# Eight transformer layers on one core: the boundaries between sublayers, taken token half by token half

## The chip, the cores and the metric

One core of a Trainium2 chip runs the whole program in one launch. The metric is the device time of one execution in microseconds (us), the median over runs. TensorE (PE) multiplies matrices, VectorE (DVE), ScalarE (ACT) and GpSimd (POOL) do the elementwise work, SyncE (SP) issues most of the transfers.

## What is computed

A residual stream x of 256 tokens by 1024 floats passes through ten sublayers, k = 0 to 9, all in float32. Sublayers 0 to 5 are two blocks of feed-forward, token mixer, feed-forward:

```
h = rms_norm(x, g_pre) * (1 + scale) + shift
y = sublayer(h)
x = x + res_w * (1 + gate) * rms_norm(y, g_post)
```

Sublayers 6 to 9 are attention, mixture of experts (MoE), attention, MoE. Their residual has no second norm:

```
h = rms_norm(x, g) * (1 + scale) + shift
x = x + gate * sublayer(h)
```

A feed-forward is (silu(h @ w_gate) * (h @ w_up)) @ w_down with a width of 2816; the mixers hold three kinds of attention and an output projection; the MoE has 16 experts of width 512, of which each token takes 2, and its router needs h of all tokens. Scale, shift and gate are vectors, made by a product of a second input with the "ada" weights.

## The kernel before

The 256 tokens are two halves t = 0, 1 of 128 rows each (NT = 2), which is also how `x[:, t, :]` lies in memory. All weights come as one stream of chunks of 1 MB (128 by 2048 floats) into six `stage` buffers. ACT makes the rounded high part of a chunk (`hi`, L578) and DVE the rest (`lo`, L1048), and each product is three matmuls on 512 columns (`mm3`, L1828, L1831, L1832). A high/low pair takes one of PARTS = 3 places, so `hi(n)` waits until PE is through with chunk n - 3.

A *column chunk* holds half of the contraction of a projection; `columns` takes it in 4 `mm3` groups for each token half, so 12 matmuls for each half and 24 in all. A *row chunk* (feed-forward down, output projection) is used by `rows`: for each token half t, 12 matmuls into the two PSUM banks `acc[2t]`, `acc[2t+1]`. When the last row chunk is done for t = 0, PE signals `half_done`.

At a boundary between sublayers k - 1 and k the engines do this, in the order in which their programs are written out (each engine is in order, nothing is scheduled at run time):

- **ACT** squares `acc` of t = 0 and of t = 1 to sums (L616, `pair<-acc`, sublayers 0 to 5 only), then x of t = 0 (L616, `pair<-x_tok`), then writes `x * rs` of t = 0 to `tok` in two parts (`by_root`, L964), then squares x of t = 1, and takes the high parts of h (`high(r)`, L980). `hi` of the next sublayer's second chunk was made before all this (`ahead`).
- **POOL** turns each sum into rs = (sum + eps) ** -0.5, by L550 and L553.
- **DVE** multiplies acc by the gate row (L1732, L1744), adds it to x (L1734, L1745), first t = 0, then t = 1; then for the four rounds r = 2t + half it takes the transposed quarter of x from PSUM with scale and shift (`scaled(r)`, L1687) and makes the low part (`rest(r)`, L1696), with `lo` of the second chunk between rounds 2 and 3.
- **PE** transposes `tok` in four rounds (`norm_round`, L1844). Three are in front of the first column matmul and the fourth is behind the first 12 matmuls (`normed`). Then come chunk 0 with both token halves and chunk 1 with both.

The last block of a feed-forward multiplies silu and product (L649, L1189), is transposed (L1892), is split in parts (L661, L1194), and is then taken by the last row chunk. Ahead of it, all of the row chunk before is done, both halves.

An MoE layer reads its chunks as float32 without a split, 96 of them, through twelve places: `stage` and the space of `w_hi` and `w_lo` (`w_raw`). Chunk 12 is loaded when PE has freed chunk 0 (`expert_chunk`). In its last expert pair ACT and DVE make parts of the next sublayer's first chunk between the last silu and the last results (`hi(end)`, L578, in `moe`).

SP issues the transfers in the order of the stream and waits at each for a free place; in the feed-forwards the slices of the ada weights (1 MB each) are laid between the chunks.

## Time and profile before

| what | value |
|---|---|
| median of 3 runs | 2297.01 us (2294.2 to 2298.27) |
| the profiled execution's own time | 2283.29 us |
| its span in the profile | 2281.3 us |
| PE busy | 2049.3 us, 90% of the span |
| DVE, ACT, POOL busy | 1438.7, 848.0, 67.6 us |
| L1048 `lo`, 240 times | 547.6 us |
| transfers | 592.53 MB, mean 260 GB/s |

A time line row reads: start in us from the span's start, duration in us, engine, line, operation, written tile <- read tiles, shapes, count; in brackets the idle time of the engine in front of it and what ended that. Rows that follow one another on one engine are merged (x2, x8), so a merged duration is that of the whole group. In matmul rows the duration covers the pipeline; the spacing of starts is what counts.

### The profile page before, as it was taken

How to read it: one execution, taken by the hardware profiler on the slowest of the kernel's cores; microseconds unless marked ns; L12 is line 12 of the kernel's file. 1: busy time of each engine (PE TensorE's matmuls, PEld its weight loads, DVE VectorE, ACT ScalarE, POOL GpSimd, SP SyncE). 2: the span in 40 equal slices, each digit the busy share in tenths (PEclk: the TensorE clock that was granted, in tenths of full speed). 3: DMA queues.
4: the chain of work that ended last, by engine and by line, in shares of the span. 5: the costliest groups of instructions: out<-in, count | busy, mean ns of one | idle time of the engine just before them, and what ended most of it. 6: DMA issues, size and time to landing. Idle time of an engine off the chain costs nothing.

```text
span 2281.3 us, 26827 instructions
## 1 busy us (share of the span) xinstructions
PE 2049.3 (90%) x9772; PEld 1513.4 (66%) x9772; DVE 1438.7 (63%) x2212; ACT 848.0 (37%) x1037; POOL 67.6 (3%) x93
## 2 busy tenths in 40 slices
PE   2999899988999899899988999886899879879997
PEld 2778788866887688778876788665544337654442
DVE  6888676656887888776656898676511137652111
ACT  3333545544343434554564433542200025321000
POOL 0000000000000000000000000110000001000000
PEclk9999999999999999999998999987999989999999
DMA  8999344334887699444432898341599985239997
GB/s 343 383 361 379 134 172 141 136 110 189 332 356 304 253 357 372 185 176 150 141 116 98 331 375 356 136 143 62 209 415 422 421 331 200 104 131 418 421 421 304
DMA packets 86332, 592.53 MB, mean 260 GB/s; under 512 B 9680, under 2 KB 13136, under 8 KB 15568
## 3 DMA queue, kind: packets, MB, share of 16 engines
q1 hardware_dynamic: 79760, 579.90, 64.3%
q10 hardware_dynamic: 6464, 11.15, 1.5%
q8 instruction: 73, 1.20, 0.2%
q14 instruction: 35, 0.29, 0.0%
HBM read 589.96 MB, written 1.05 MB: 259 GB/s over the span
## 4 chain that ended last, share of the span: by engine, by line
PE 71%; DMA 11%; DVE 10%; ACT 4%; issue 2%; POOL 1%; SPq 0%; ACTq 0%; DVEq 0%; POOLq 0%
PE acc L1828 12%; PE acc L1832 11%; PE acc L1831 11%; PE gu L2130 8%; PE gu L1828 6%; PE gu L1832 6%; PE gu L1831 6%; DMA w_raw<-wstream 5%; PE tr L2130 4%; DMA stage<-wstream 3%; PE acc L2130 3%; PE tr L1892 3%; DVE w_lo L1048 2%; DMA proj<-ada_stream 2%; DVE tf L1687 1%
## 5 line engine op out<-in xcount | busy, mean ns | idle before, releaser
L1048 DVE TENSOR_TENSOR w_lo<-stage,w_hi 128x2048 fp32r<-128x2048 f32 x240 | 547.6, 2286 | 68.0 <-ACT w_hi L578 67.9
L578 ACT ACTIVATE w_hi<-stage 128x2048 fp32r<-128x2048 f32 x240 | 457.4, 1911 | 279.1 <-PE acc L1832 261.3
L1120 DVE SCALAR_TENSOR_TENSOR proj<-proj,c_row 128x1024 f32<-128x1024 f32 x240 | 291.5, 1218 | 53.4 <-DMA proj<-ada_stream 44.7
L1828 PE MATMUL acc<-w_hi,hT_hi 128*128 128x512 f32 (+1 forms) x736 | 308.6, 419 | 5.1 <-DVE hT_lo L1392 5.1
L1828 PE MATMUL gu<-w_hi,hT_hi 128*128 128x512 f32 x704 | 283.8, 403 | 11.1 <-DVE pair L1189 10.8
L1831 PE MATMUL acc<-w_lo,hT_hi 128*128 128x512 f32 (+1 forms) x736 | 292.0, 397 | 0.0
L1832 PE MATMUL acc<-w_hi,hT_lo 128*128 128x512 f32 (+1 forms) x736 | 291.9, 397 | 0.0
L1832 PE MATMUL gu<-w_hi,hT_lo 128*128 128x512 f32 x704 | 277.7, 394 | 0.0
L1831 PE MATMUL gu<-w_lo,hT_hi 128*128 128x512 f32 x704 | 277.5, 394 | 0.0
L1828 PE MATMUL acc<-w_hi,yT_hi 128*128 128x512 f32 (+1 forms) x460 | 183.8, 400 | 14.0 <-DVE yT_lo L1604 5.7
L2130 PE MATMUL gu<-stage,got 128*64 128x512 f32 x768 | 170.6, 594 | 15.0 <-DMA stage<-wstream 15.0
L1832 PE MATMUL acc<-w_hi,yT_lo 128*128 128x512 f32 (+1 forms) x460 | 180.3, 392 | 0.0
L1831 PE MATMUL acc<-w_lo,yT_hi 128*128 128x512 f32 (+1 forms) x460 | 180.1, 392 | 0.0
L1828 PEld LDWEIGHTS acc<-w_hi,hT_hi 128*128 128x128 f32 x736 | 142.7, 194 | 43.2 <-issue 10.6
L1828 PEld LDWEIGHTS gu<-w_hi,hT_hi 128*128 128x128 f32 x704 | 134.6, 191 | 42.4 <-DVE pair L1189 12.9
L1832 PEld LDWEIGHTS acc<-w_hi,hT_lo 128*128 128x128 f32 x736 | 142.0, 193 | 30.6
L1831 PEld LDWEIGHTS acc<-w_lo,hT_hi 128*128 128x128 f32 x736 | 142.8, 194 | 26.3 <-issue 1.0
L1832 PEld LDWEIGHTS gu<-w_hi,hT_lo 128*128 128x128 f32 x704 | 134.1, 190 | 29.1
L1831 PEld LDWEIGHTS gu<-w_lo,hT_hi 128*128 128x128 f32 x704 | 134.7, 191 | 26.6
L2130 PEld LDWEIGHTS gu<-stage,got 128*64 128x64 f32 x768 | 60.0, 137 | 121.9 <-issue 108.7
L1844 PE MATMUL tr<-const,tok 128*128 128x128 f32 x160 | 36.8, 387 | 100.3 <-ACT tok L964 89.8
L1279 DVE TENSOR_TENSOR pair<-pair,gu 128x256 f32<-128x256 f32 x32 | 13.5, 421 | 171.7 <-ACT pair L689 171.7
(221 smaller groups left out, 2449.0 us busy)
## 6 DMA issues: line engine op xcount, KB each, us to landing
stage<-wstream SPq DMA_DIRECT2D x336, 1024.0 KB, 5.3
proj<-ada_stream SPq DMA_DIRECT2D x120, 1024.0 KB, 7.7
w_raw<-wstream SPq DMA_DIRECT2D x96, 1024.0 KB, 18.0
tf<-bgate_in ACTq DMA_DIRECT2D x12, 256.0 KB, 4.3
proj<-rel_in ACTq DMA_DIRECT2D x16, 192.0 KB, 2.3
proj<-t_in ACTq DMA_DIRECT2D x8, 192.0 KB, 3.4
z_mix<-c_in ACTq DMA_DIRECT2D x2, 512.0 KB, 7.7
x_tok<-x_in ACTq DMA_DIRECT2D x1, 1024.0 KB, 19.8
```

Source lines behind the costliest of these rows:

```text
L578: act.activation(w_hi[:, n % PARTS, :], stage[:, n % STAGES, :], ACT.Copy).then_inc(hi_ready, 1)
L1048: dve.tensor_tensor(w_lo[:, n % PARTS, :], stage[:, n % STAGES, :], w_hi[:, n % PARTS, :].bitcast(F32), ALU.subtract).then_inc(chunk_ready, 1)
L1120: ins = dve.scalar_tensor_tensor(w, w, 1.0, c_row[:], ALU.mult, ALU.mult, accum_out=dst)
L1279: dve.tensor_tensor(both[:, j, BLK:2 * BLK], both[:, j, 0:BLK], gu[:, j, BLK:2 * BLK], ALU.mult).then_inc(both_ready, 1)
L1687: ins = dve.tensor_scalar(tf[:, (b["tf"] + r) % 2, j * P:(j + 1) * P], tr[:, (b["u"] + r) % 2, j * P:(j + 1) * P], mod[:, 3 * k + 1, c:c + ...
L1828: ins = pe.matmul(dst, l_hi, r_hi, start=start, stop=False, skip_group_check=True)
L1831: pe.matmul(dst, l_hi, r_lo, start=False, stop=False, skip_group_check=True)
L1832: return pe.matmul(dst, l_lo, r_hi, start=False, stop=stop, skip_group_check=True)
L1844: ins = pe.transpose(tr[:, (u + r) % 2, j * P:(j + 1) * P], tok[:, 1 - t, c * P:(c + 1) * P], ident)
L1892: ins = pe.transpose(tr[0:rows_, u % 2, j * P:(j + 1) * P], src, ident)
L2130: return pe.matmul(dst, lhs, rhs, start=start, stop=stop, skip_group_check=True)
```

## The change

The residual and the norm of token half 0 now run ahead of those of half 1, and both ends of PE's work are sorted by token half.

1. **End of a feed-forward** (`ffn` on PE, last block written out): of the last two row chunks, t = 0 is taken of both first, then t = 1 of both. The hidden block's transposes stand in the middle of the first chunk's t = 0, 6 matmuls ahead of them and 6 behind; the parts go to a place of their own (`end_hi`, `end_lo`). ACT's and DVE's parts of the last chunk are made ahead of the last silu. The output projection ("out") is sorted in the same way: chunks 0 and 1 whole, then t = 0 of 2 and 3, then t = 1 of 2 and 3. `half_done` now comes 24 matmuls ahead of the end, where it was 12.
2. **Residual** (`residual`, `mean_square`, `row_root`): squares, gate product and addition in halves of 512, with new semaphores `acc_read` and `x_part`; POOL adds the two sums. Half 1's residual is no longer in front of the norm: DVE does it between `scaled(0)` and `scaled(1)`, with `rest(0)` inside, ACT squares it behind `by_root(0)`. `lo` of the second chunk stands in front of `rest(1)`, behind a wait for POOL's root of half 1. ACT makes that chunk's high part in two halves between these steps.
3. **First column chunks** (`first_columns`, sublayers 1, 2, 3, 4, 5, 6, 8): two transpose rounds, chunk 0 with t = 0, round 2, chunk 1 with t = 0, round 3, then both chunks with t = 1. The `norm` in front of an MoE has no column chunks; it still gets the new order of residual and norm.
4. **MoE**: two more places, used once each, for chunks 12 and 13 (`once`, in `z_mix` and in `prob` and its neighbours); chunk 14 waits until chunk 2 is free. Parts of the next sublayer's first chunk are made behind the last results (ACT) and in front of `scaled(0)` (DVE).
5. **Start**: the first chunk is loaded one ada slice later and its `lo` stands behind `scaled(0)`.

```diff
+        slot = n % STAGES
+        if c and RING <= c[0] < RING + ONCE:
+            slot = c[0]
+        elif c and c[0] % RING >= STAGES:
+            slot = c[0] % RING
...
+        end_hi = yT_hi[:, 2:4, :].rearrange("p a s -> p (a s)")
+        end_lo = yT_lo[:, 2:4, :].rearrange("p a s -> p (a s)")
...
+        once = [z_mix[:].rearrange("p t c -> p (t c)"), nc.alloc_sbuf_tensor_at("once", [P, CW], F32, offset=prob_at)[:]]
...
+            if RING <= n - n0 < RING + ONCE:
+                return once[n - n0 - RING]
...
-                if m >= NORM_SLICES - 2 and n < 8:
+                if m >= NORM_SLICES - 1 and n < 8:
...
-                for c in range(RING):
+                for c in range(2 * RING):
                     expert_chunk(n0 + c, n0)
-                with sp.Fori(0, PAIRS - 1) as i:
+                with sp.Fori(0, PAIRS - 2) as i:
                     for c in range(RING):
-                        expert_chunk(n0 + RING + c, n0, i)
+                        expert_chunk(n0 + 2 * RING + c, n0, i)
...
+            def row_root(request, at):
+
+                nonlocal ups
+                pool.wait_ge(rs_req, request)
+                pool.tensor_scalar(ss[:, at:at + 1], ss[:, at:at + 1], ss[:, at + 8:at + 9], EPS, ALU.add,
+                                   ALU.add).then_inc(pool_up, 1)
+                ups += 1
+                pool.wait_ge(pool_up, ups)
+                pool.tensor_tensor(rs[:, at:at + 1], ss[:, at:at + 1], mhalf[:, at:at + 1], ALU.pow).then_inc(rs_done, 1)
...
+                if kind == "norm":
+                    row_root(norm_request(b, step[1], 0), 0)
+                    if 1 <= step[1] <= 6:
+                        row_root(resid_request(plan[at - 1][1], 1), NT + 1)
+                    row_root(norm_request(b, step[1], 1), 1)
+                elif kind == "resid" and step[1] < 6:
+                    row_root(resid_request(b, 0), NT)
...
-                    hi(n + 1)
...
+            def mean_square(request, at, halves, parts=None, read=None):
+
+                if request > 1:
+                    act.wait_ge(rs_req, request - 1)
+                for h in range(2):
+                    if parts:
+                        act.wait_ge(x_ready if h else x_part, parts)
+                    ins = act.activation(both[:, h, :], halves[h], ACT.Square, scale=D ** -0.5,
+                                         accum_out=ss[:, at + 8 * h:at + 8 * h + 1])
+                    if h == 0 and read is not None:
+                        ins.then_inc(read, 1)
+                ins.then_inc(rs_req, 1)
+
+            def row_halves(t):
+                return [x[:, t, 512 * h:512 * h + 512] for h in range(2)]
+
+            def gated_square(b, k, t):
+
+                act.wait_ge(pe_used, b["n"] + PARTS) if t else act.wait_ge(half_done, k + 1)
+                mean_square(resid_request(b, t), NT + t, [acc[:, 2 * t + h, :] for h in range(2)], read=acc_read)
...
+                hi(n0 + 3 * nb - 1)
                 silu(nb - 1)
-                hi(n0 + 3 * nb - 1)
-                turn_hi(nb - 1, hidden_turn(b["u"], nb - 1))
+                act.wait_ge(tr_full, hidden_turn(b["u"], nb - 1) + 1)
+                act.wait_ge(pe_used, n0 + 1 + PARTS)
+                act.activation(end_hi, tr[:, hidden_turn(b["u"], nb - 1) % 2, :], ACT.Copy).then_inc(th_ready, 1)
                 ahead(n0 + 3 * nb)
...
-                    if p == PAIRS - 1 and end < n_chunks:
-                        act.wait_ge(chunk_ready, moe_up_at(n0, p, 1, 1, 1) + 1)
-                        hi(end)
                     y_high(p, 0)
                     y_high(p, 1)
-                if end < n_chunks:
-                    act.wait_ge(chunk_ready, end + 1)
-                    hi(end + 1)
+                act.wait_ge(chunk_ready, end)
+                ahead(end)
...
-                        act.wait_ge(x_ready, NT * (k - 1) + 1)
-                        mean_square(b, 0, x[:, 0, :], 0)
-                        by_root(b, 0)
-                        act.wait_ge(x_ready, NT * (k - 1) + 2)
-                        mean_square(b, 1, x[:, 1, :], 1)
-                    high(0)
-                    if k:
-                        by_root(b, 1)
-                    high(1)
+                        mean_square(norm_request(b, k, 0), 0, row_halves(0), NT * (k - 1) + 1)
+                        if chunks:
+                            hi_half(b["n"] + 1, 0)
+                        by_root(b, k, 0)
+                        if k <= 6:
+                            gated_square(plan[at - 1][1], k - 1, 1)
+                        high(0)
+                        if chunks:
+                            hi_half(b["n"] + 1, 1)
+                        mean_square(norm_request(b, k, 1), 1, row_halves(1), NT * (k - 1) + 2)
+                        high(1)
+                        by_root(b, k, 1)
+                    else:
+                        high(0)
+                        hi(1)
+                        high(1)
                     high(2)
-                    if k < 3 * DEPTH or (k - 3 * DEPTH) % 2 == 0:
+                    if chunks:
                         hi(b["n"] + 2)
                     high(3)
...
-                if m == NORM_SLICES - 1:
-                    lo(0)
...
+                lo(n0 + 3 * nb - 1)
                 silu(nb - 1)
-                lo(n0 + 3 * nb - 1)
-                turn_lo(nb - 1)
+                turn_lo(nb - 1, to=(end_hi, end_lo))
                 ahead(n0 + 3 * nb)
...
+            def residual(k, b, t, after=None, between=None):
+
+                nonlocal ups
+                gated, row = tok[:, 1 - t, :], x[:, t, :]
+                for h in range(2):
+                    c = slice(512 * h, 512 * h + 512)
+                    if k < 6:
+                        dve.wait_ge(rs_req, resid_request(b, t)) if h else dve.wait_ge(acc_read, NT * k + t + 1)
+                    elif t == 0:
+                        dve.wait_ge(half_done, k + 1)
+                    elif k % 2:
+                        dve.wait_ge(whole_done, (k - 3 * DEPTH) // 2 + 1)
+                    else:
+                        dve.wait_ge(pe_used, b["n"] + PARTS)
+                    dve.tensor_tensor(gated[:, c], acc[:, 2 * t + h, :], tok[:, 0, c], ALU.mult).then_inc(dve_up, 1)
+                ups += 2
+                if between:
+                    between()
+                if k < 6:
+                    dve.wait_ge(rs_done, resid_request(b, t))
+                if after:
+                    dve.wait_ge(rs_done, norm_request(after, k + 1, 0))
+                for h in range(2):
+                    c = slice(512 * h, 512 * h + 512)
+                    dve.wait_ge(dve_up, ups - 1 + h)
+                    if k < 6:
+                        ins = dve.scalar_tensor_tensor(row[:, c], gated[:, c], rs[:, NT + t:NT + t + 1], row[:, c],
+                                                       ALU.mult, ALU.add)
+                    else:
+                        ins = dve.tensor_tensor(row[:, c], row[:, c], gated[:, c], ALU.add)
+                    ins.then_inc(x_ready if h else x_part, 1)
...
+                    if k == 3 * DEPTH + 2:
+                        dve.wait_ge(chunk_ready, b["n"])
+                        lo(b["n"])
                     scaled(0)
-                    rest(0)
-                    scaled(1)
-                    scaled(2)
-                    rest(1)
-                    rest(2)
-                    if k < 3 * DEPTH or (k - 3 * DEPTH) % 2 == 0:
+                    if k == 0:
+                        lo(0)
+                        rest(0)
+                        scaled(1)
+                        scaled(2)
+                        rest(1)
+                        rest(2)
                         lo(b["n"] + 1)
+                    else:
+                        residual(k - 1, plan[at - 1][1], 1, between=lambda: rest(0))
+                        scaled(1)
+                        dve.wait_ge(rs_done, norm_request(b, k, 1))
+                        if k < 3 * DEPTH or (k - 3 * DEPTH) % 2 == 0:
+                            lo(b["n"] + 1)
+                        rest(1)
+                        scaled(2)
+                        rest(2)
                     scaled(3)
                     rest(3)
...
+                    residual(k, b, 0)
+                    if k == NSUB - 1:
+                        residual(k, b, 1)
...
+            def first_columns(b, dst, width=512):
+
+                for t in range(NT):
+                    for part in range(2):
+                        r = 2 * t + part
+                        pe.wait_ge(tr_free, b["u"] - 1 + r)
+                        columns(b["n"] + part, dst, 4 * part, 4, part == 0, part == 1, width, only=(t,))
+                        if t == 0:
+                            norm_round(b["u"] - 4, b["tf"] - 4, 2 + part, b["src"] - 4)
...
+                with pe.Fori(0, turns - 1) as i:
                     block_(1 + peeled, i)
                     block_(2 + peeled, i)
-                turn_hidden(nb - 1)
-                down(n0 + 3 * nb - 1, nb - 1, False, True)
+                g = nb - 1
+                block_(g - 1)
+                up(n0 + 3 * g - 1, 0, g)
+                turn_hidden(g - 1)
+                up(n0 + 3 * g, 1, g)
+
+                def of(hi_part, lo_part):
+                    return lambda k, t: tuple(v[:, (2 * k + t) * P:(2 * k + t + 1) * P] for v in (hi_part, lo_part))
+
+                prev, last = n0 + 3 * g + 1, n0 + 3 * g + 2
+                pe.wait_ge(tr_free, hidden_turn(b["u"], g - 1) + 1 + 2)
+                chunk_wait(prev)
+                row_part(prev, 0, (0,), of(hid_hi, hid_lo), False)
+                turn_hidden(g)
+                row_part(prev, 0, (1,), of(hid_hi, hid_lo), False)
+                pe.wait_ge(tr_free, hidden_turn(b["u"], g) + 1 + 2)
+                chunk_wait(last)
+                row_part(last, 0, (0, 1), of(end_hi, end_lo), True).then_inc(half_done, 1)
+                row_part(prev, 1, (0, 1), of(hid_hi, hid_lo), False).then_inc(pe_used, 1)
+                row_part(last, 1, (0, 1), of(end_hi, end_lo), True).then_inc(pe_used, 1)
...
-                    for c in range(4):
+                    def of(c):
+                        return lambda k, t: tuple(v[:, 2 * c + k, t * P:(t + 1) * P] for v in (hT_hi, hT_lo))
+
+                    for c in range(2):
                         pe.wait_ge(tr_free, b["u"] + c - 1)
-                        rows(b["n"] + c, lambda k, t: tuple(v[:, 2 * c + k, t * P:(t + 1) * P] for v in (hT_hi, hT_lo)),
-                             c == 0, c == 3)
-                        if c == 1:
-                            gate_row(b, b["u"])
+                        rows(b["n"] + c, of(c), c == 0, False)
+                    gate_row(b, b["u"])
+                    for t in range(NT):
+                        for c in range(2, 4):
+                            if t == 0:
+                                pe.wait_ge(tr_free, b["u"] + c - 1)
+                                chunk_wait(b["n"] + c)
+                            ins = row_part(b["n"] + c, t, (0, 1), of(c), c == 3)
+                            if t:
+                                ins.then_inc(pe_used, 1)
+                        if t == 0:
+                            ins.then_inc(half_done, 1)
```

How this moves DVE's instructions at the boundary between the first output projection and the second feed-forward. `acc` and `x_tok` are the residual, `tf` and `hT_lo` the norm, `w_lo` the chunk's low part. Before:

```order
L1732 TENSOR_TENSOR tok<-acc,tok 128x1024 [waits rs_req,dve_up]
L1734 SCALAR_TENSOR_TENSOR x_tok<-tok,rs,x_tok 128x1024 [waits rs_done,dve_up]
L1732 TENSOR_TENSOR tok<-acc,tok 128x1024 [waits rs_req]
L1734 SCALAR_TENSOR_TENSOR x_tok<-tok,rs,x_tok 128x1024 [waits rs_done,dve_up]
L1687 TENSOR_SCALAR tf<-tr,mod 128x128 [waits tr_full]
L1687 TENSOR_SCALAR tf<-tr,mod 128x128 x3
L1696 TENSOR_TENSOR hT_lo<-tf,hT_hi 128x4x128 [waits th_ready]
L1687 TENSOR_SCALAR tf<-tr,mod 128x128 [waits tr_full]
```

Now, from the first norm round on (half 0's residual is done ahead of these rows):

```order
L1773 TENSOR_SCALAR tf<-tr,mod 128x128 [waits tr_full]
L1773 TENSOR_SCALAR tf<-tr,mod 128x128 x3
L1743 TENSOR_TENSOR tok<-acc,tok 128x512 [waits acc_read]
L1743 TENSOR_TENSOR tok<-acc,tok 128x512 [waits rs_req]
L1782 TENSOR_TENSOR hT_lo<-tf,hT_hi 128x4x128 [waits th_ready]
L1755 SCALAR_TENSOR_TENSOR x_tok<-tok,rs,x_tok 128x512 [waits dve_up,rs_done]
L1755 SCALAR_TENSOR_TENSOR x_tok<-tok,rs,x_tok 128x512 [waits dve_up]
L1773 TENSOR_SCALAR tf<-tr,mod 128x128 [waits tr_full]
L1773 TENSOR_SCALAR tf<-tr,mod 128x128 x3
L1110 TENSOR_TENSOR w_lo<-stage,w_hi 128x2048 [waits hi_ready,rs_done]
L1782 TENSOR_TENSOR hT_lo<-tf,hT_hi 128x4x128 [waits th_ready]
```

Half 1's product and addition have moved from in front of the norm to between its first two rounds, and the chunk's low part to in front of the second `hT_lo`.

On SP, at the first MoE, the transfers behind the six `stage` ones, now:

```order
L509 DMA w_raw<-wstream 128x2048 [waits pe_used] x6
L509 DMA z_mix<-wstream 128x2048 [waits pe_used]
L509 DMA once<-wstream 128x2048 [waits pe_used]
L509 DMA stage<-wstream 128x2048 [waits chunk_ready] x4
L509 DMA w_raw<-wstream 128x2048 [waits chunk_ready] x6
```

Before, the six of `w_raw` were the last that did not wait for a chunk of the MoE itself; now two more stand in front of that wait.

## Rows read from the trace of the kernel before

**Rows 1.** waits of the whole span: who waited for whom, us, times, longest

```profile
PE tr L1844 <- ACT tok L964: 89.8, 19, 29.3
```

**Rows 2.** timeline, first feed-forward to first mixer: start us, us, engine line op tiles [idle]

```profile
240.10 1.03 ACT L616 ACTIVATE pair<-acc 128x1024 f32<-128x1024 f32 x1 [0.25 <-PE acc L1832]
...
241.60 0.57 POOL L553 TENSOR_TENSOR rs<-ss,mhalf 128x1 f32<-128x1 f32 x1
...
242.57 1.28 DVE L1734 SCALAR_TENSOR_TENSOR x_tok<-tok,rs,x_tok 128x1024 f32<-128x1024 f32 x1
...
245.56 1.38 POOL L553 TENSOR_TENSOR rs<-ss,mhalf 128x1 f32<-128x1 f32 x1
246.98 1.33 ACT L964 ACTIVATE tok<-x_tok,rs 128x512 f32<-128x512 f32 x2 [1.81 <-POOL rs L553]
...
247.75 1.97 PE L1844 MATMUL tr<-const,tok 128*128 128x128 f32 x8 [4.97 <-ACT tok L964]
...
248.91 1.36 DVE L1687 TENSOR_SCALAR tf<-tr,mod 128x128 f32<-128x128 f32 x4 [2.39 <-PE tr L1844]
...
252.37 0.69 PE L1828 MATMUL acc<-w_hi,hT_hi 128*128 128x416 f32 x1
...
262.70 0.35 PE L1832 MATMUL acc<-w_hi,hT_lo 128*128 128x416 f32 x1
```

**Rows 3.** timeline, end of the last dense feed-forward, VectorE and TensorE

```profile
1427.13 0.69 DVE L1189 TENSOR_TENSOR pair<-pair,gu 128x512 f32<-128x512 f32 x1 [3.36 <-ACT pair L649]
...
1431.74 0.60 PE L1892 MATMUL tr<-const,pair 128*128 128x128 f32 x4
1433.75 0.50 PE L1828 MATMUL acc<-w_hi,yT_hi 128*128 128x512 f32 x1 [1.41 <-DVE yT_lo L1194]
```

**Rows 4.** timeline, VectorE: two copies of half a row, merged

```profile
98.35 1.28 DVE L1098 COPY tok<-tr 128x512 f32<-128x512 f32 x2
```

**Rows 5.** timeline, output projection and boundary before the second feed-forward

```profile
526.10 0.79 PE L1828 MATMUL acc<-w_hi,hT_hi 128*128 128x512 f32 x1
...
537.20 0.39 PE L1832 MATMUL acc<-w_hi,hT_lo 128*128 128x512 f32 x1
...
527.31 4.48 DVE L1048 TENSOR_TENSOR w_lo<-stage,w_hi 128x2048 fp32r<-128x2048 f32 x2
...
560.33 0.39 PE L1832 MATMUL gu<-w_hi,hT_lo 128*128 128x512 f32 x1
```

**Rows 6.** timeline, attention heads to first router

```profile
1603.03 1.23 DVE L1744 TENSOR_TENSOR tok<-acc,tok 128x1024 f32<-128x1024 f32 x1 [1.95 <-PE acc L1832]
...
1607.10 1.50 POOL L553 TENSOR_TENSOR rs<-ss,mhalf 128x1 f32<-128x1 f32 x1
...
1619.23 0.69 DVE L1696 TENSOR_TENSOR hT_lo<-tf,hT_hi 128x512 fp32r<-128x512 f32 x1 [0.70 <-ACT hT_hi L980]
```

**Rows 7.** stretches of us: PE, PEld, DVE, ACT, POOL busy, PEclk, DMA share, GB/s

```profile
548.20:551.10 2.90, 2.90 (x8) 2.28 (x7) 2.80 (x6) 2.25 (x3) 0.00 (x0) 0.50 0.02 6
...
57.00:93.00 36.00, 33.18 (x138) 26.32 (x139) 29.59 (x47) 14.74 (x11) 0.00 (x0) 0.95 0.98 401
1622.00:1640.00 18.00, 15.01 (x98) 10.55 (x98) 11.30 (x44) 4.03 (x8) 0.00 (x0) 1.00 0.01 5
1640.00:1866.00 226.00, 204.22 (x1020) 88.01 (x1016) 43.40 (x77) 22.93 (x36) 0.00 (x0) 0.99 1.01 418
```

**Rows 8.** timeline, ends of the two expert layers; L1744 starts when half the rows are done

```profile
1853.16 3.65 PE L2130 MATMUL tr<-w_raw,hidT 128*64 128x512 f32 x16 [0.43 <-DMA w_raw<-wstream]
...
1862.57 1.22 DVE L1744 TENSOR_TENSOR tok<-acc,tok 128x1024 f32<-128x1024 f32 x1 [1.16 <-PE acc L2130]
...
2265.05 3.65 PE L2130 MATMUL tr<-w_raw,hidT 128*64 128x512 f32 x16 [0.38 <-DMA w_raw<-wstream]
...
2271.17 1.23 DVE L1744 TENSOR_TENSOR tok<-acc,tok 128x1024 f32<-128x1024 f32 x1 [0.90 <-PE acc L2130]
```

**Rows 9.** timeline, start of the program

```profile
34.38 2.29 DVE L1048 TENSOR_TENSOR w_lo<-stage,w_hi 128x2048 fp32r<-128x2048 f32 x1 [3.62 <-ACT w_hi L578]
```

121 lines of the change are left out of this document (58 added, 63 removed).

## The prediction

> **What bounds the kernel.** I read the table of waits first. The largest wait of TensorE for another engine is that of its transposes for ScalarE's scaled rows: 89.8 us in 19 waits, of which 29.3 are the start of the program [rows 1]. That is the boundary between sublayers, where TensorE is idle while residual and norm are made. The time line of the first boundary shows the chain [rows 2]. ScalarE squares the first half at 240.10, so half_done is at 239.9. The sum of x is squared only when the square of the other half is out of the way; its root on POOL takes 1.38 us, where the one at 241.60 took 0.57, because VectorE is adding x of half 1 (in rows 6 a root takes 1.50 beside the same addition). Rows are scaled at 246.98, transposed at 247.75, scaled again at 248.91, and the first column matmul starts at 252.37: 12.5 us after half_done. The first two column chunks end at 262.9, 23.0 us after half_done. The second boundary has 512 columns instead of 416. Its output projection's last 48 matmuls start from 526.10 to 537.20 [rows 5]; without 0.4 at the first that is 0.228 us each, they end at 537.4, and half_done is 12 matmuls ahead, at 534.7. The two column chunks end at 560.6 [rows 5]: 25.9 after half_done. TensorE is 90% busy on the page, so what a boundary gives should be kept. In the MoE it is otherwise: DMA moves 418 GB/s at a share of 1.01 from 1640 to 1866 [rows 7], and the last expert matmuls wait for their weights [rows 8].
>
> **Feed-forward end, 4 times.** The last transposes start at 1431.74, and the last chunk only at 1433.75, with 1.41 us idle for the parts [rows 3]. Now six matmuls (1.36 us) cover this. The 24 matmuls ahead of 1431.74 begin at 1426.3, so the first six end at 1427.7, and the transposes wait for the product that ends at 1427.82 [rows 3]: 0.2 us, and some 0.1 remains of the other wait. Saved: 1.41 - 0.25 = 1.15, times 4 = **-4.6**. VectorE's low part of the next chunk (2.29) and three small operations now lie behind the parts and end about 1.2 us after half_done, which delays the first product by 0.1.
>
> **Boundaries with columns after sublayers 0 to 5.** half_done moves from 12 to 24 matmuls ahead of the end, so it comes 2.73 us earlier. From half_done on, by the durations of rows 2 and half-width ones of 0.6 between starts [rows 4]: two squares with their accumulator reads 1.6, root 0.9 (from the square's end, 241.3, to 242.2), additions 1.3, two squares behind the first of these 4.8, root 5.7 (VectorE is idle, so 0.87 and not 1.7), scaled row 6.5, transposes 7.5, scaling 8.9, two gate products 10.2, low part and first matmul **10.9** (was 12.4). But then VectorE is in the way: two additions to 12.1, scaling 13.4, the root of half 1 at 14.0, the chunk's low part (2.29) 16.3, second low part **16.9**. There chunk 1's 12 matmuls for half 0 start; before, TensorE ran on without this stop. They end at 19.7, round 3 follows, VectorE scales 20.4 to 21.7, parts to 23.2, and the last 12 matmuls end at **25.9**. That is what it was (25.9), so with 512 columns the boundary saves the 2.73 alone.
> - After sublayers 2 and 5: 2.73 - 0.1 - 0.1 = 2.5, times 2 = **-5.0**.
> - After 1 and 4 (output projection): the last chunk is needed 12 matmuls earlier, at 526.10 + 0.4 + 2.73 = 529.2, and its low part is ready at 527.31 + 2.25 = 529.6 [rows 5]; with the gate row's copies in front, 0.6 is lost. 2.73 - 0.1 - 0.6 = 2.0, times 2 = **-4.0**.
> - After 0 and 3 (416 columns): matmuls are shorter but VectorE's chain is not; the end comes at 25.0 after half_done instead of 23.0. 2.73 - 2.0 - 0.1 = 0.6, times 2 = **-1.2**.
>
> What halving costs: two halves take 1.28 us of VectorE where one whole takes 1.22 [rows 4, 8], so 0.06 a split, which the steps above hold. The Trainium skill (VectorE: DVE Perf Modes, section "The TRN2 errata — SBUF-src ops pay a fixed extra latency per instruction") says that each instruction pays a fixed term, by its formula (N + 151) / 0.96 ns 0.16 us more for two halves. By it, six splits on a boundary's path would cost 0.6 us more than my sum, 5 us over nine boundaries.
>
> **Attention to MoE, twice.** No columns are behind this norm: the router needs all four rounds, so only the end of round 3 counts. Before it ends 16.9 us after the first product starts (1603.03 to 1619.92 [rows 6]). x of half 1 was ready after two products and two additions, at 5.1; now it is added behind scaled(0) and two products, at 10.5. From there: two squares 11.5, root 12.4, row 13.2, transposes 14.2, scaling 15.6, parts 17.1, scaling 18.3, parts **19.8**. Nothing is gained in exchange, since half_done stays where it is. 2.9, times 2 = **+5.8**. It is not hidden, since the first expert matmul, and with it the next transfer, waits for the router.
>
> **The MoE's two places, twice.** Transfers rest from 1622 to 1640 (5 GB/s [rows 7]), and two chunks of 1.05 MB are 5.0 us at 418 GB/s. But the queue now goes on when chunk 2 is free, not chunk 0, one group of 16 matmuls (3.65 us [rows 8]) later. 5.0 - 3.6 = 1.4, times 2 = **-2.8**, as TensorE waits for weights at the end.
>
> **End of the first MoE.** From the start of the last 16 expert matmuls to the first gate product it is 9.41 us, and 6.12 in the second MoE, which has no next chunk to convert [rows 8]: -3.3. At this boundary chunk 0's low part (2.29) now lies in front of scaled(0); it runs while POOL makes the root, which costs 0.8 as beside an addition (1.38 against 0.57 [rows 2]) and, I take, 0.4 at the root's first step. The stop in front of chunk 1 costs 1.0 more, as this sublayer's half_done is near its end before and after. **-1.1** in all.
>
> **Start.** VectorE was idle 3.62 us and busy 2.29 with a chunk ahead of the first norm [rows 9]; about 2.3 us of this go. But every chunk is loaded one ada slice later and DMA is full from 57 to 93 (401 GB/s [rows 7]): one more chunk (2.5 us) is left to load when it starts. I take **0**, bounds +1 and -2.3. The halves of the last residual: +0.1.
>
> **Sum:** -4.6 - 5.0 - 4.0 - 1.2 + 5.8 - 2.8 - 1.1 + 0.1 = **-12.8 us**, so 2283.3 of the profiled execution becomes 2270.5. The median of the runs is 13.7 above that execution; the difference carried over gives 2297.0 - 12.8 = **2284.2**.
>
> **Rivals.**
> - *Slower: the clock.* The new order trades one long idle time for several short ones: 8.5 to 10.9, 13.7 to 16.9 after half_done. Matmuls of 512 columns start every 0.41 us where the granted clock is 0.50, which is 1.2 of 2.4 GHz (8 in 2.90 us [rows 7]), against 0.23. If the clock stays low over the next 24 matmuls, each of seven boundaries loses 24 x 0.2 = 4.8 us, less some 1.5 that VectorE's stops hide: +23, or 2307. From four such boundaries on nothing is left of the gain. For it: the clock is low behind the boundary's idle time (PEclk 0.50 [rows 7]). Against it: there TensorE had been idle 4.97 us [rows 2], now it is 1.1 us until the transposes and then 2.4 and 3. The Trainium skill (TensorE: Matmul & The Clock Gate, section "HAM oscillation — how this bites in real kernels") says that bursts of work with waits between them can make the clock fall at each burst anew. By that rule the loss would come at every one of the seven boundaries. The MoE, which also works in bursts between waits, has 0.99 from 1640 to 1866 [rows 7]. Chance 8%.
> - *No change: VectorE's chain is longer than its rows.* If scaled(0) to the last low part takes 1.5 us more than summed at the seven column boundaries (waits for banks, roots blocked beside VectorE's chunk parts), -12.8 + 10.5 = -2.3: 2294.7. 14%.
> - *Faster: full price.* If transfers of the MoE's two chunks count fully (5.0 each, the queue does not starve behind chunk 2) and the start keeps 2.3: -12.8 - 7.2 - 2.3 = -22.3, 2274.7. For it: chunks come free faster than they load. Against: the rest of the stream still starts at chunk 2. 13%.
> - *It doesn't do what it says.* If the early half_done is worth nothing because ScalarE still converts a chunk then: at the feed-forward ends it now has one chunk (1.9 us) less to convert there, which the diff puts ahead of the squares (`ahead`). With half_done's gain lost at four boundaries it is -12.8 + 10.9: 2295.1. 3%.
>
> **Chances.** Forecast 62%. A measurement tells about 0.2%, 4.6 us, from no change: faster is below 2292.4. Forecast and third rival hold 0.75, and the better ends of the second and fourth 0.03 more: 0.78. The rest of these two is no change, 0.14, and the clock slower, 0.08. Range: the unknown costs are the start (+1, -2.3), VectorE's chain (+10.5), the clock in part (+5) and the MoE (-7.2); with a fifth left out it is 2274 to 2295.
>
> **What would show it.** First column matmul about 10.9 us after half_done and a new stop of 1 to 3 us in front of chunk 1's first matmul; the 1.41 us in front of the feed-forward's last chunk gone; the router's norm ending 3 us later than before, counted from the first product; DMA busy some 5 us longer before the MoE and a root of 0.9 instead of 1.7 us. I am wrong if the first columns end more than 27 us after half_done, if the router's norm is not later, or if the MoE's stretch from first expert matmul to last is shorter by more than 6 us in all besides the 3.3 of its end.

## The result and the profile after

| | before | after |
|---|---|---|
| median of six runs, us | 2294.16 (2291.10 to 2298.27) | 2283.64 (2276.59 to 2285.06) |
| profiled execution, its own time / span, us | 2283.29 / 2281.3 | 2283.56 / 2281.8 |
| mean granted clock of that execution | 0.966 | 0.963 |

The ratio of the runs is 0.9948, with a 95% interval of 0.9932 to 0.9964: 11.9 us (8.3 to 15.6) less, where 12.8 were forecast. The two profiled executions show none of it. That of before was 11 us under its kernel's median, so a second profile of before was needed to compare by (e1 below). One of the twelve executions of e4 ran at a mean clock of 0.558 and took 3484 us; no ratio counts it. The page of after:

```profile
PE 2061.6 (90%) x9772; PEld 1517.3 (66%) x9772; DVE 1443.1 (63%) x2252; ACT 854.9 (37%) x1108; POOL 64.1 (3%) x93
PE tr L1928 <- ACT tok L1021: 59.3, 12, 29.7
```

The second line is from the table of waits and answers to [rows 1]: TensorE's transposes wait for the scaled rows 12 times instead of 19, and 59.3 us instead of 89.8. Not all of that is gain, since the new order has stops of its own, ahead of the column matmuls, which this row doesn't count. The boundary behind sublayer 1 (the first with 512 columns), from the time lines of ScalarE, VectorE and TensorE (start, duration; in brackets the idle time before and what ended it). The first square starts at 539.83, so half_done is at 539.6:

```profile
539.83 0.60 ACT L663 ACTIVATE pair<-acc 128x512 f32<-128x512 f32 x1 [5.82 <-PE acc L1916]
...
542.18 1.42 DVE L1755 SCALAR_TENSOR_TENSOR x_tok<-tok,rs,x_tok 128x512 f32<-128x512 f32 x2 [0.27 <-POOL rs L584]
...
546.22 1.27 PE L1928 MATMUL tr<-const,tok 128*128 128x128 f32 x8 [0.98 <-ACT tok L1021]
546.91 1.37 DVE L1773 TENSOR_SCALAR tf<-tr,mod 128x128 f32<-128x128 f32 x4 [3.31 <-PE tr L1928]
548.20 1.28 DVE L1743 TENSOR_TENSOR tok<-acc,tok 128x512 f32<-128x512 f32 x2
549.99 1.41 DVE L1755 SCALAR_TENSOR_TENSOR x_tok<-tok,rs,x_tok 128x512 f32<-128x512 f32 x2
550.17 0.47 PE L1912 MATMUL gu<-w_hi,hT_hi 128*128 128x512 f32 x1 [2.69 <-issue]
...
553.24 2.29 DVE L1110 TENSOR_TENSOR w_lo<-stage,w_hi 128x2048 fp32r<-128x2048 f32 x1 [0.56 <-POOL rs L584]
556.19 0.50 PE L1912 MATMUL gu<-w_hi,hT_hi 128*128 128x512 f32 x1 [0.99 <-DVE hT_lo L1782]
...
565.13 0.39 PE L1916 MATMUL gu<-w_hi,hT_lo 128*128 128x512 f32 x1
```

After half_done the first column matmul starts at +10.5 (forecast 10.9), chunk 1's first matmul at +16.6 (16.9), after a stop of 0.99, and the 48 matmuls end at +25.8 (25.9). GpSimd's root of x is done 0.9 us after it starts, as forecast, where it took 1.7 before. The answer to [rows 3], the last transposes of a feed-forward, from TensorE's time line:

```profile
1425.35 0.39 PE L1916 MATMUL acc<-w_hi,yT_lo 128*128 128x512 f32 x1
1425.79 0.66 PE L1998 MATMUL tr<-const,pair 128*128 128x128 f32 x4
1426.20 0.47 PE L1912 MATMUL acc<-w_hi,yT_hi 128*128 128x512 f32 x1
...
1427.44 0.40 PE L1916 MATMUL acc<-w_hi,yT_lo 128*128 128x512 f32 x1
1427.86 0.50 PE L1912 MATMUL acc<-w_hi,yT_hi 128*128 128x512 f32 x1
```

The 1.41 us are gone; about 0.2 is left on either side of the transposes and the six matmuls.

**Where the time went.** Stages of the second profile of before (e1, span 2293.3) against the profile of after, each read from the start of a matmul in the two traces. Both have the mixers in the same form (explained under e1), so they can be set side by side. The rows of the forecast are rounded; unrounded they add up to 12.8.

| stage | before (e1) | after | difference | forecast |
|---|---|---|---|---|
| start to first square of boundary 0 | 240.92 | 241.63 | +0.7 | -3.9 |
| from there to the end of its first columns | 22.88 | 24.52 | +1.6 | +2.1 |
| first heads and mixer | 249.03 | 248.98 | 0.0 | 0 |
| output projection and boundary 1 | 53.99 | 51.80 | -2.2 | -2.0 |
| feed-forward and boundary 2 | 201.82 | 198.35 | -3.5 | -3.7 |
| feed-forward and boundary 3 (416 columns) | 200.75 | 195.73 | -5.0 | -1.7 |
| second heads and mixer | 246.78 | 246.85 | +0.1 | 0 |
| output projection and boundary 4 | 53.93 | 51.82 | -2.1 | -2.0 |
| feed-forward and boundary 5 | 200.17 | 196.71 | -3.5 | -3.7 |
| the two attention sublayers, together | 275.29 | 272.99 | -2.3 | 0 |
| last product to routing, two layers | 31.69 | 37.89 | +6.2 | +5.8 |
| routing to end, first MoE | 241.99 | 239.06 | -2.9 | -4.7 |
| boundary behind the first MoE | 24.60 | 25.88 | +1.3 | +2.2 |
| routing to end, second MoE | 249.48 | 249.55 | +0.1 | -1.3 |
| **sum** | | | **-11.5** | **-12.8** |

The sum is nearly right. Three kinds of rows are not: the start, the MoE stretches, and stages that the change doesn't touch or touches less than they gained. Of the last, much belongs to this one profile of before: its other profile has 198.2 us in the feed-forward with boundary 3 and 273.8 in the attention sublayers, so that against it they gained 2.4 and 0.8 us and not 5.0 and 2.3.

### The profile page after: what moved, and what is told of

It reads as the page before. It is cut to its first block, busy times and chain, and to the rows that moved or that the text cites. A ratio compares the mean times of both kernels' runs of the same rounds, so it can differ in the third digit from the quotient of the medians.

```text
span 2281.8 us, 26854 instructions
## 1 busy us (share of the span) xinstructions
PE 2061.6 (90%) x9772; PEld 1517.3 (66%) x9772; DVE 1443.1 (63%) x2252; ACT 854.9 (37%) x1108; POOL 64.1 (3%) x93
## 3 DMA queue, kind: packets, MB, share of 16 engines
q8 instruction: 78, 1.28, 0.2%
## 4 chain that ended last, share of the span: by engine, by line
PE 69%; DVE 11%; DMA 11%; ACT 5%; issue 3%; POOL 1%; SPq 0%; ACTq 0%; DVEq 0%; POOLq 0%
PE acc L1912 11%; PE acc L1916 10%; PE acc L1915 10%; PE gu L2259 9%; PE gu L1912 6%; PE gu L1916 6%; PE gu L1915 6%; DMA w_raw<-wstream 5%; PE tr L2259 5%; PE acc L2259 3%; PE tr L1998 3%; DVE w_lo L1110 2%; DMA stage<-wstream 2%; DMA proj<-ada_stream 2%; DVE tf L1773 1%
## 5 line engine op out<-in xcount | busy, mean ns | idle before, releaser
L613 ACT ACTIVATE w_hi<-stage 128x2048 fp32r<-128x2048 f32 x233 | 444.5, 1911 | 276.4 <-PE acc L1916 252.4
L1182 DVE SCALAR_TENSOR_TENSOR proj<-proj,c_row 128x1024 f32<-128x1024 f32 x240 | 292.2, 1221 | 50.9 <-DMA proj<-ada_stream 40.6
L2259 PE MATMUL gu<-stage,got 128*64 128x512 f32 x736 | 163.5, 594 | 15.0 <-DMA stage<-wstream 15.0
L1912 PEld LDWEIGHTS gu<-w_hi,hT_hi 128*128 128x128 f32 x704 | 134.8, 191 | 60.6 <-DVE pair L1249 16.9
L2259 PEld LDWEIGHTS gu<-stage,got 128*64 128x64 f32 x736 | 57.1, 137 | 117.7 <-issue 104.3
L2259 PE MATMUL tr<-w_raw,hidT 128*64 128x512 f32 x512 | 114.3, 596 | 4.7 <-DVE got L1321 3.0
## 6 DMA issues: line engine op xcount, KB each, us to landing
once<-wstream SPq DMA_DIRECT2D x2, 1024.0 KB, 19.8
```

Of the source, the lines that this page charges most:

```text
L613: act.activation(w_hi[:, n % PARTS, :], stage[:, n % STAGES, :], ACT.Copy).then_inc(hi_ready, 1)
L1182: ins = dve.scalar_tensor_tensor(w, w, 1.0, c_row[:], ALU.mult, ALU.mult, accum_out=dst)
L1912: ins = pe.matmul(dst, l_hi, r_hi, start=start, stop=False, skip_group_check=True)
L2259: return pe.matmul(dst, lhs, rhs, start=start, stop=stop, skip_group_check=True)
```

## The experiments

All are timed in interleaved runs against the kernel before. After's own ratio is 0.9948, and 0.9950 (0.9936 to 0.9965) when it was measured again (e5). The intervals of e2, e3 and e4 each touch or overlap after's, so they need their traces beside them; e7, which has the edits of e2 and e3 together, is clear of it.

### e1: the kernel before again

> The kernel before, unchanged, as a control: its own ratio to itself, and what the profiled execution of before (span 2281.3 us at a mean granted clock of 0.966) has to do with its median of 2294. Theory 1 (the clock): executions of one program differ because TensorE is granted 1.2 GHz in more or fewer stretches; then the runs of this kernel show mean clocks of about 0.960 where the span is 2292, 0.966 where it is 2281, about 1.8 us for each 0.001. Theory 2 (the time around the span, or transfers): the runs at 2292 show the same 0.966, and the trace differs in waits for DMA. Ratio 1.000 within 0.002 in both.

2293.06 us, ratio 1.0004 (0.9991 to 1.0017). Its profile has a span of 2293.3 at a clock of 0.959, against 2281.3 at 0.966: 12.0 us for 0.007, or 1.7 us per 0.001. The largest single piece is the end of the first mixer (245.18 us in one profile, 249.03 in the other). Windows of 22 us shortly before that end, of before, of e1 and of after (they close 3.1, 3.8 and 7.1 us ahead of it; us, busy time of PE, PEld, DVE, ACT, POOL, then PEclk, DMA share, GB/s):

```profile
483.00:505.00 22.00, 16.17 (x73) 12.94 (x72) 9.02 (x13) 9.41 (x9) 0.00 (x0) 0.92 0.13 48
```

```profile
487.00:509.00 22.00, 17.18 (x57) 13.43 (x58) 5.71 (x11) 8.15 (x8) 0.00 (x0) 0.69 0.14 48
```

```profile
486.00:508.00 22.00, 16.17 (x56) 12.59 (x55) 6.36 (x9) 7.74 (x8) 0.00 (x0) 0.69 0.13 48
```

The same stretch of code runs at 0.92 or at 0.69: 73 matmuls fall in 22 us, or 56 and 57 (60 in e1 and in after if their windows close 3 us ahead of the end too). The second profile of after (e5) has 0.92 here and 245.18 us. Theory 1 holds for the mixer: these are not two kernels, but two outcomes of the same code. It holds for whole executions too: over 74 of them of the kernel before, the median time is 2298.9 us where the mean clock is 0.955, 2291.2 where it is 0.960, and the one execution at 0.965 took 2284.1. The profiled execution of before that the forecast was read from had the better one in several places. This is why the two profiled spans agree while the medians differ by 11 us, and why the forecast rightly started from the median and not from that execution.

### e2: the loads of the start one slice earlier

```
-                if m >= NORM_SLICES - 1 and n < 8:
+                if m >= NORM_SLICES - 2 and n < 8:
```

> The changed kernel with its chunk loads at the start one slice earlier, as before; the low part of chunk 0 stays behind scaled(0). Theory A (the loads): in the changed kernel SyncE's queue issues chunk 4 at 54.00 instead of 39.35, since it stands behind a slice that waits for VectorE's sums; VectorE then waits 5.45 us for it, and the copy of the gate row comes 4.8 us later than before. With the loads back the copy is where it was (98.4) or up to 3 us earlier, and the kernel is 4.8 to 8 us faster than the changed one: ratio to before 0.991 to 0.993. Theory B (the forecast's: DMA is full anyway and the loads cost nothing): no change beyond 1 us, ratio 0.995.

2274.52 us, ratio 0.9928 (0.9913 to 0.9942): 5 us under the changed kernel by the ratios. The half_done of boundary 0 is at 234.5 instead of 241.6 (239.2 in e5's profile). In the six profiles with after's start and feed-forward end it lies at 237.6 to 241.6, in the three with this edit (e2, e7, e9) at 233.4 to 235.3. SyncE's rows of after, then of before, then of e2:

```profile
53.63 0.33 SPq L497 DMA_DIRECT2D proj<-ada_stream  x1
54.00 0.43 SPq L488 DMA_DIRECT2D stage<-wstream  x1
```

```profile
38.98 0.33 SPq L476 DMA_DIRECT2D proj<-ada_stream  x1
39.35 0.44 SPq L467 DMA_DIRECT2D stage<-wstream  x1
```

```profile
35.79 0.33 SPq L497 DMA_DIRECT2D proj<-ada_stream  x1
36.16 0.43 SPq L488 DMA_DIRECT2D stage<-wstream  x1
```

All three are the load of chunk 4. And VectorE in after, which needs it:

```profile
64.15 2.29 DVE L1110 TENSOR_TENSOR w_lo<-stage,w_hi 128x2048 fp32r<-128x2048 f32 x1 [5.45 <-ACT w_hi L613]
```

SyncE's queue stands 17 to 19 us (39.8 to 57.1 before, 34.3 to 53.6 after) at a slice whose place VectorE frees only after the first norm. With one chunk fewer issued ahead of it, chunk 4 starts 14.7 us later. Theory A holds, theory B (the forecast's) falls.

### e3: the norms in front of the MoE in the old order

```
-                    else:
+                    elif k in (3 * DEPTH + 1, 3 * DEPTH + 3):
+                        rest(0)
+                        scaled(1)
+                        scaled(2)
+                        rest(1)
+                        rest(2)
+                    else:
                         residual(k - 1, plan[at - 1][1], 1, between=lambda: rest(0))
...
-                    if k == NSUB - 1:
+                    if k in (NSUB - 1, 3 * DEPTH, 3 * DEPTH + 2):
                         residual(k, b, 1)
```

and ScalarE's order to match.

> The changed kernel with the old order at the two norms in front of the MoE (residual of half 1 ahead of the norm of half 0). The forecast priced this at 2.9 us each; the traces show the router's norm 2.65 and 3.55 us longer. Theory A: both come back in full, -6.0 us against the changed kernel, ratio to before 0.992; last expert transfers start 3 us earlier. Theory B (hidden behind the transfers of the experts' weights, which are loaded ahead): the norm is 3 us shorter in the trace but the MoE takes as much longer, ratio 0.995.

2271.98 us, ratio 0.9919 (0.9902 to 0.9936): about 7 us under the changed kernel by the ratios, and the two stretches from the last matmul of the output projection to the routing take 14.61 us each instead of 18.72 and 19.17 (16.08 and 15.61 in e1). Theory A. TensorE in after (first fence) and in e3:

```profile
1601.68 1.36 PE L1928 MATMUL tr<-const,tok 128*128 128x128 f32 x8 [2.58 <-ACT tok L1021]
1609.44 1.97 PE L1928 MATMUL tr<-const,tok 128*128 128x128 f32 x8 [6.40 <-ACT tok L1021]
```

```profile
1597.62 1.42 PE L1939 MATMUL tr<-const,tok 128*128 128x128 f32 x8 [2.58 <-ACT tok L1021]
1601.27 2.31 PE L1939 MATMUL tr<-const,tok 128*128 128x128 f32 x8 [2.24 <-ACT tok L1021]
```

There is a second part that I had not foreseen. The routing behind the norm (from its first transpose to the first expert matmul) took 14.0 us before and takes 16.6 now. Windows over it, before and after:

```profile
1621.00:1635.30 14.30, 10.99 (x80) 9.57 (x80) 10.85 (x46) 4.30 (x9) 0.00 (x0) 1.00 0.09 38
```

```profile
1617.00:1634.00 17.00, 13.58 (x80) 12.19 (x80) 10.97 (x46) 4.40 (x9) 0.00 (x0) 0.80 0.22 93
```

The same 80 matmuls at a granted clock of 0.80 instead of 1.00, behind an idle time of 6.40 us. In e3 it is 15.5 us at 0.89. In the second layer the steps are 15.2, 16.6 and 15.4. The idle time alone does not decide it, though. Over all thirteen profiles, the 14 routings behind an idle time of 6.0 us or more took 16.6 to 17.7 us ten times, 15.3 to 15.4 three times (both of e6) and 13.8 once (the second layer of e11); the 12 routings in the old order took 13.8 to 14.0 four times, 15.2 to 15.5 seven times and 16.5 once (e9). The means are 16.2 and 15.0, so the new order costs about 1.2 us in each layer here on average, and the 2.6 above compares one of the quickest with one of the slow ones.

### e4: without the two extra places

```
-ONCE = 2
+ONCE = 0
```

and SyncE's loops from chunk 12 on, as before.

> The changed kernel without the two extra places for the MoE's chunks. The forecast gives them 1.4 us in each of the two layers: the time rises by 2.8 us, ratio to before 0.996. Rival A (they are worth the two transfers in full): it rises by 10, ratio 0.999. Rival B (they are worth nothing, as the trace suggests: from the routing to the last instruction the second MoE takes 249.6 us with them and 249.0 before): no change within 1 us, ratio 0.995, and DMA is less busy in front of the MoE and as much longer in it.

2285.51 us, ratio 0.9974 (0.9961 to 0.9987): some 6 us over the changed kernel by the ratios, whose intervals touch. In the 36 us ahead of the first expert matmul, after has moved 2.1 MB more than e4, which is the two chunks. From the first expert matmul to the last, where that can be worth something, the two layers take 220.5 and 220.9 us in e4, and 219.4 and 220.6 in after: +1.0 and +0.3. From the last product to the end of the first MoE it is +2.5, but 1.1 of that is a routing at a clock of 0.75, beside 0.79, and 0.4 the norm. So the traces show 1.3 for the places, less than the forecast's 2.8, and the runs about 6, give or take 4. Rival A's 10 isn't borne out by the traces and B's zero not by the runs; the size is not settled.

### e5 and e6: half_done late again

```
+                row_part(prev, 1, (0, 1), of(hid_hi, hid_lo), False).then_inc(pe_used, 1)
                 row_part(last, 0, (0, 1), of(end_hi, end_lo), True).then_inc(half_done, 1)
-                row_part(prev, 1, (0, 1), of(hid_hi, hid_lo), False).then_inc(pe_used, 1)
                 row_part(last, 1, (0, 1), of(end_hi, end_lo), True).then_inc(pe_used, 1)
```

> The changed kernel unchanged, on the same chip as the three that follow, so that their ratios can be set against its own: 0.995 as in the first measurement. Both theories of the clock agree here; its trace shows how far two profiles of this kernel differ in the stretches at 1.2 GHz (172 us in the first).

> The changed kernel with the last 24 matmuls of the feed-forward ends in the old order: half 1 of the last chunk but one goes ahead of half 0 of the last, so half_done is 12 matmuls (2.73 us) nearer the end at four boundaries. The six matmuls ahead of the transposes stay. Theory A (the forecast: the boundary's chain starts at half_done and nothing hides it): +2.6 at each, +10.4 us, ratio to before 0.9995. Theory B (VectorE's chain sets the boundary anyway, so half_done gives half or less): +5 or less, ratio 0.997. If theory C holds, that the longer idle also keeps the clock low for longer, it is more than +12, ratio over 1.000.

e5: 2281.71 us. e6: 2292.02, ratio 0.9991 (0.9981 to 1.0001), so +10.3 by the medians and 9.4 by the ratios. By the runs that is theory A: a boundary is worth what half_done gains, 2.6 us here. The clock does stay low for longer, as theory C has it (windows under e10), and the traces show a cost of it that the total hides. The stretches that hold a feed-forward with boundary 2, 3 and 5 are 3.2 us longer than in after, not 2.6. TensorE at boundary 2 in e6, where half_done is at 739.97 (after's rows at a boundary are above, at 546.22 and 550.17):

```profile
746.54 1.97 PE L1928 MATMUL tr<-const,tok 128*128 128x128 f32 x8 [3.69 <-ACT tok L1021]
750.96 0.77 PE L1912 MATMUL gu<-w_hi,hT_hi 128*128 128x512 f32 x1 [2.45 <-issue]
```

The eight transposes take 1.97 us instead of 1.27, and the first column matmul comes 11.0 us after half_done and not 10.5. That is theory C's effect, about 0.5 at three of the four boundaries. In the same profile both routings were of the 15.3 us kind where after has 16.6, which gives 2.6 back.

### e7 and e8: a version that beats both

e7 is after with e2's and e3's edits together. e8 has e3's edit, and of the start's loads two behind the first slice that allows them instead of each one slice earlier.

> The changed kernel with both: chunk loads of the start one slice earlier, and the old order at the norms in front of the MoE. Theory A (the two are independent): the loads give 5 to 7 us and the routers 8 to 10, together 13 to 17 under the changed kernel, ratio to before 0.988 to 0.989. Theory B (part of what each showed was the chip's clock of that moment): 8 to 10 us, ratio 0.991.

> As the kernel with both, but chunks 0 and 1 are loaded one behind the other right behind the slice that the first norm needs, so that the first norm waits for no chunk and chunk 4 is still issued before the queue blocks. Theory A: the first column matmul starts at 39 as in the changed kernel (40.6 with the loads back), and 1.6 us more are kept: ratio 0.0007 lower. Theory B (DMA is full until 93, so the order of the first transfers makes no difference by the first boundary): same time within 1 us.

e7: 2264.78 us, ratio 0.9873 (0.9857 to 0.9889), 29 us under before and 17 under after. e8: 2265.22, 0.9881 (0.9865 to 0.9897), the same. In e8 the first column matmul starts at 39.0 instead of 40.6 and boundary 0 comes 3.8 us earlier in its profile, but the runs don't show it.

### e9: gate products of half 1 ahead of scaled(0)

```
+                    if 1 <= k <= 6:
+                        def first():
+                            scaled(0)
+                            rest(0)
+                        residual(k - 1, plan[at - 1][1], 1, between=first, early=True)
```

where `early` makes the products wait for the sums alone, and ScalarE's squares wait for the products.

> The kernel with loads and routers back (0.9873 of before), and in it at the six boundaries after sublayers 0 to 5 one more edit: VectorE makes the two gate products of half 1 ahead of scaled(0), in the 3.3 us in which it is idle there, straight from the sums, and ScalarE squares them behind that. In the changed kernel x of half 1 is added only at 549.99, since products and root come behind scaled(0). Theory A (VectorE's chain sets the boundary): x of half 1 is ready 1.0 us earlier and with it the end of the first columns, 6 x 1.0 = 6 us, ratio to before 0.9845 to 0.985. Theory B (ScalarE's squares now wait and the root is made beside VectorE's additions, or the first half's root is slowed beside the products): first column matmul later by what half 1 gains, ratio 0.987.

2267.45 us, ratio 0.9891 (0.9872 to 0.9910): no gain over e7, to which this edit was made. VectorE in e9; ScalarE's first square is at 530.46:

```profile
537.55 1.37 DVE L1785 TENSOR_SCALAR tf<-tr,mod 128x128 f32<-128x128 f32 x4 [0.36 <-PE tr L1959]
539.62 0.69 DVE L1794 TENSOR_TENSOR hT_lo<-tf,hT_hi 128x512 fp32r<-128x512 f32 x1 [0.69 <-ACT hT_hi L1042]
540.22 1.41 DVE L1767 SCALAR_TENSOR_TENSOR x_tok<-tok,rs,x_tok 128x512 f32<-128x512 f32 x2
```

x of half 1 is added 9.8 us behind that square, against 10.2 in after: 0.4 earlier and not 1.0, because the low part of round 0 now stands in front of it. I had moved the products off the chain and left the next link out of the sum. Six times 0.4 is below what these runs can tell.

### e10: the first two chunks one after the other again

```
-                for t in range(NT):
-                    for part in range(2):
...
+                norm_round(b["u"] - 4, b["tf"] - 4, 2, b["src"] - 4)
+                for part in range(2):
+                    for t in range(NT):
```

> The changed kernel, but TensorE takes the first two column chunks chunk by chunk again (round 2 of the transposes ahead of the first column matmul), while half_done, VectorE's and ScalarE's order stay. Theory A (summed from the trace: round 2 is done at 555.2 instead of the first matmul at 550.17, then 24 matmuls, round 3 and 24 matmuls without a stop): first columns end 1.5 to 2 us later at each of seven boundaries, +11 to +14 us, ratio to before 1.000. Theory B (VectorE's chain ends last in either order): +3 or less, ratio 0.996. In both TensorE is idle from 548 to 554, over 5 us in one piece again, so if the clock gains from the split idle time, the stretches at 1.2 GHz at the boundaries are 10.2 us instead of 3.4.

2295.38 us, ratio 1.0013 (0.9999 to 1.0026): about 15 us over after by the ratios, 12 to 14 by the medians. In the profile the seven boundaries are longer by 1.9 us (416 columns and behind the MoE) to 2.8 us (512 columns), 16 us in all. Early sums are worth nothing if TensorE's order holds the first matmul back for round 2: in the new order of VectorE, the half-by-half order of TensorE carries at least as much as the early half_done. It is not that the old kernel lost this much by its order: there all of x was ready sooner, and the first column matmul came 12.5 us after half_done, where in e10 it comes after 15.2. TensorE in e10:

```profile
552.69 1.08 PE L1928 MATMUL tr<-const,tok 128*128 128x128 f32 x4 [6.57 <-ACT tok L1021]
```

And windows of 10 us over boundary 2, where transposes and first columns are (they open 7.3 us after half_done in before, 8.0 in after and e6, 10.0 in e10): before, after, e6, e10.

```profile
745.00:755.00 10.00, 7.61 (x31) 6.06 (x32) 7.78 (x16) 7.06 (x10) 0.79 (x2) 0.66 0.00 1
```

```profile
746.00:756.00 10.00, 6.51 (x23) 4.99 (x23) 9.17 (x17) 5.25 (x12) 1.72 (x4) 0.83 0.10 21
```

```profile
748.00:758.00 10.00, 7.13 (x23) 5.26 (x22) 9.44 (x19) 5.04 (x11) 1.72 (x4) 0.62 0.08 13
```

```profile
749.00:759.00 10.00, 5.52 (x17) 4.51 (x18) 7.96 (x14) 5.64 (x10) 0.86 (x2) 0.54 0.29 102
```

After has 0.83 where before has 0.66. With the idle time in front of the transposes longer (e6, 3.69 us) or in one piece of 6.57 us (e10) the clock is at 0.62 and 0.54. One boundary of one profile is a single draw, however. From 8 to 18 us after half_done, the boundaries behind sublayers 0 to 5 show 0.55 to 0.68 in the two profiles of before (12 boundaries), 0.55 to 0.69 in e10 (6), and 0.83 or 0.66 in the eight profiles whose code there is after's: 27 times the one and 21 times the other. Even after itself has 0.66 at two of its six. The order between the kernels stands, the single value doesn't. Nor does the better value give time at such a boundary: with 0.66 (e5, boundary 1) the first columns end 25.7 us after half_done and with 0.83 (after) 25.7 as well; what differs is that at 0.66 TensorE didn't stop in front of chunk 1.

### e11: end of the first MoE as before

The next chunk's high and low part go back in front of the last y parts.

```
                     silu(p, 1)
+                    if p == PAIRS - 1 and end < n_chunks:
+                        act.wait_ge(chunk_ready, moe_up_at(n0, p, 1, 1, 1) + 1)
+                        hi(end)
                     y_high(p, 0)
```

> The changed kernel with the end of the first MoE as before: next chunk's high and low part ahead of the last y parts. Forecast: 3.3 us back at the end of the expert matmuls, 2.2 us less at the boundary, +1.1 in all. Rival (the boundary's part is larger, 2.5 us by the traces, and DMA-bound work in front takes up the rest): within 1 us of the changed kernel. A ratio can't tell these apart (0.995 or 0.9955); the trace shows the two parts: from the last expert matmul to the last scatter 6.5 us instead of 3.0, from there to the end of the first columns 23.4 instead of 25.9.

2284.33 us, ratio 0.9964 (0.9950 to 0.9978). From the start of the last expert matmul to that of the last scatter it is 7.0 us instead of 3.0, and from there to the end of the first columns 24.6 instead of 25.9: +4.0 - 1.3 = 2.7 us. The ratios give about 3, which is within their interval of nothing. The same end took 6.5 and 7.6 us in the two profiles of before, and the same boundary 23.4 and 24.6, so both parts move by about a microsecond between profiles. TensorE in e11, then the same place in after:

```profile
1849.81 0.47 PE L2263 MATMUL acc<-yhi,pickT 128*128 128x512 f32 x1 [3.88 <-DVE ylo L1349]
```

```profile
1855.68 0.51 PE L2259 MATMUL acc<-yhi,pickT 128*128 128x512 f32 x1 [0.49 <-DVE ylo L1348]
```

## Why the prediction came out right, point by point

- **What bounds it, and the boundaries with columns: right, and shown.** half_done decides (e6: 9.4 to 10.3 us for four times 2.73, where 10.4 were expected), and each landmark of the chain fell within 0.4 us of its sum. With 512 columns the boundary gained 2.1 to 3.5 us with what belongs to it, as forecast; the 3.5 came again within 0.1 us in most other profiles, while the output projection with boundary 1 took 53.3 us in five of the nine profiles with this code and 51.8 in four, and after's 2.2 was the better draw of these. The halving cost what its rows said: two gate products take 1.28 us together, where one whole took 1.22. For the additions of sublayers 0 to 5 they said nothing, and the forecast kept 1.3: two halves take 1.41 on average, where one whole took 1.29. The Trainium skill's fixed term ("VectorE: DVE Perf Modes", section "The TRN2 errata — SBUF-src ops pay a fixed extra latency per instruction") would have made it 0.16 more, by an estimate from its formula; the rows show 0.06 and 0.12. The durations in the trace agree with that formula (0.68 us for a half product, 1.22 for a whole), but the second half starts 0.60 us behind the first.
- **Feed-forward end: right.** The 1.41 us became about 0.4, beside the six matmuls.
- **Start, "I take 0": wrong.** It cost 4.6 us by the table (+0.7 where -3.9 stood), 2.2 by e5's profile, and e2 takes back 5. The step that failed is "one more chunk (2.5 us) is left to load when it starts". I had priced the lost load as bytes on a full DMA. The queue's own wait decides: a transfer that falls behind a blocked issue waits the block out, 19.3 us in after, and so was issued 14.7 us later than before, and VectorE waited 5.45 us for it. I did not follow the queue past its next wait.
- **Attention to MoE, +5.8: the norm right, its sequel missed.** From the first product to the end of round 3 it is 19.5 us (1596.48 to 1616.01 in the trace), forecast 19.8; over both layers the norms cost 6.2. Undoing the order gives back 8.7 there, so e3, which keeps squares and additions in halves, ends 2.5 under before; which of its parts does that was not isolated. The routing behind it was 2.6 and 1.3 us longer in this profile, about 1.2 each on average over all profiles, at a lower clock. So the order costs some 9 us against before; e3 shows 7 for its undoing, and e7 against e2 10 to 13.
- **Extra places, -2.8: open.** The traces show 1.3 in the expert stretches, the runs of e4 about 6.
- **End of the first MoE, -1.1: the mechanism right, the size off.** It is worth 2.7 (e11): the end gains 4.0 instead of 3.3, and the boundary loses 1.3 instead of 2.2 (2.5 against the first profile of before).
- **The rival "slower: the clock" had the sign wrong at the column boundaries.** I asked whether several short idle times would keep the clock low. At the six boundaries behind sublayers 0 to 5 they keep it higher: 0.83 or 0.66, against 0.55 to 0.68 before (under e10). The seventh, behind the first MoE, still has 6.0 us of idle time in one piece, and over 26 us from the last scatter its clock is 0.74, before 0.75 and 0.70. I took it from the Trainium skill ("TensorE: Matmul & The Clock Gate", section "HAM oscillation — how this bites in real kernels"), that bursts between waits let the clock fall anew at each, and by that rule the loss was to come at all seven boundaries; the trace shows none. That was my use of the rule more than the page, whose example has waits of about 3 to 5 us between its bursts, where the new order's are 1.0, 2.7 and 1.0. The one stretch where the clock was lower more often with this change is the routing, behind an idle time that had grown to some 6.4 us.
- **Why the sum still held.** The unforeseen costs (start 4.6; routing 3.9) were partly made up by stages that got more than forecast in the table: boundary 3 and its feed-forward 3.3 more, the attention sublayers 2.3, where the change does nothing. Against the other profile of before these two are 0.7 and 0.8, so they are for the most part how e1's profile fell. I take them for the clock; that was not isolated by a run of its own, since the same stage differs by 2 to 4 us between two profiles of one kernel (e1). What made up for the start and the routing in the medians is therefore not shown stage by stage. The forecast was right in its mechanisms at the boundaries and somewhat lucky in its total. The nearness of the time itself (2284.2 and 2283.64) has a second piece of luck in it: before's median was 2297.01 over three runs when the forecast was made and 2294.16 over six, from which 12.8 less is 2281.4.
